# The second mixer's projection, indexer and top-k in one unrolled block

## The reference, cut to what matters

```
z = h @ w_in                      # 1024 q | 512 k,v | 512 qi | 64 ki | 8 wi
q, k, qi, ki = rope(...)          # on the first 16 of each 64 columns
score = sum_h relu(qi_h . ki / 8) * wi_h     # 8 indexer heads, causal
keep  = top_k(score, 128 of 512)  # sample rows: 64 of 257
o = softmax(q k^T / 8 over keep) v ;  x += o @ w_out
```

## Time and profile before

| | |
|---|---|
| median of 3 runs | 2544.56 us (2543.56 to 2545.28) |
| the profiled execution | 2541.22 us, of which the trace spans 2539.5 us |
| busy: PE, DVE, ACT, POOL | 2351.2, 1109.2, 712.6, 285.3 us |
| page, weight loads of the mixer | 16 of 512 KB, 3.6 us to landing |

### The profile page before, as it was taken

The page is one execution under the profiler, slowest core; times in us unless marked ns, Lnnn a source line. Parts: engine busy times, 40 slices in busy tenths (PEclk is TensorE's granted clock), DMA queues, the critical chain, the costliest instruction groups (busy, mean ns, idle before and its releaser), DMA issues. The chain is left out here.

```text
span 2539.5 us, 43612 instructions
## 1 busy us (share of the span) xinstructions
PE 2351.2 (93%) x17356; PEld 2121.0 (84%) x17356; DVE 1109.2 (44%) x1802; ACT 712.6 (28%) x1179; POOL 285.3 (11%) x356
## 2 busy tenths in 40 slices
PE   6999999988799889999999999999964989999997
PEld 5999998766644689999998999997742468999997
DVE  5433433222477435434434433433277744443434
ACT  2221222222255123222223222222241513222220
POOL 1000002000255120000020000011040412000002
PEclk8999999997899999999999999999976989999998
DMA  3332332225300222332332332332201012332331
GB/s 101 91 102 81 91 102 65 82 63 182 117 18 1 67 67 83 95 96 86 96 91 75 91 100 83 91 100 67 79 28 56 12 29 80 91 102 81 91 102 56
DMA packets 327479, 202.44 MB, mean 80 GB/s; under 512 B 11698, under 2 KB 306666, under 8 KB 327322
## 3 DMA queue, kind: packets, MB, share of 16 engines
q1 hardware_dynamic: 323226, 199.10, 26.6%
q10 hardware_dynamic: 4160, 2.10, 0.3%
HBM read 194.65 MB, written 10.70 MB: 81 GB/s over the span
## 5 line engine op out<-in xcount | busy, mean ns | idle before, releaser
L156 DVE TENSOR_TENSOR w_lo<-w_stage,w_hi 128x1024 fp32r<-128x1024 f32 (+1 forms) x266 | 350.9, 1319 | 850.2 <-ACT w_hi L149 850.2
L149 ACT ACTIVATE w_hi<-w_stage 128x1024 fp32r<-128x1024 f32 (+1 forms) x266 | 301.9, 1135 | 761.5 <-PE y_ps L163 371.2
L161 PE MATMUL gate_ps<-h_hi,w_hi 128*128 128x260 f32 x1408 | 404.2, 287 | 27.0 <-DVE h_lo L184 19.7
L163 PE MATMUL gate_ps<-h_hi,w_lo 128*128 128x260 f32 x1408 | 402.8, 286 | 0.0
L162 PE MATMUL gate_ps<-h_lo,w_hi 128*128 128x260 f32 x1408 | 401.7, 285 | 0.0
L161 PE MATMUL up_ps<-h_hi,w_hi 128*128 128x260 f32 x1408 | 398.2, 283 | 0.0
L161 PE MATMUL y_ps<-a_hi,w_hi 128*128 128x260 f32 x1408 | 397.9, 283 | 0.0
L163 PE MATMUL up_ps<-h_hi,w_lo 128*128 128x260 f32 x1408 | 397.8, 283 | 0.0
L163 PE MATMUL y_ps<-a_hi,w_lo 128*128 128x260 f32 x1408 | 397.5, 282 | 0.0
L162 PE MATMUL y_ps<-a_lo,w_hi 128*128 128x260 f32 x1408 | 397.4, 282 | 0.0
L162 PE MATMUL up_ps<-h_lo,w_hi 128*128 128x260 f32 x1408 | 396.4, 282 | 0.0
(11 more groups left out here) (425 smaller groups left out, 3246.0 us busy)
## 6 DMA issues: line engine op xcount, KB each, us to landing
w_stage<-w_ffn_in SPq DMA_DIRECT2D x176, 512.0 KB, 3.8
w_stage<-w_ffn_out SPq DMA_DIRECT2D x64, 704.0 KB, 4.5
w_stage<-w_nsa_in SPq DMA_DIRECT2D x20, 512.0 KB, 3.5
w_stage<-w_dsa_in SPq DMA_DIRECT2D x16, 512.0 KB, 3.6
w_stage<-w_nsa_out SPq DMA_DIRECT2D x8, 512.0 KB, 3.5
cmp_page<-cache_nsa_cmp SPq DMA_DIRECT2D x16, 256.0 KB, 3.9
nsa_win_rows<-state_nsa_win SPq DMA_DIRECT2D x16, 256.0 KB, 3.7
w_stage<-w_dsa_out SPq DMA_DIRECT2D x8, 512.0 KB, 3.7
```

Source lines behind the costliest of these rows:

```text
L149: act.activation(e.w_hi[slot][:, 0:cols], e.w_stage[slot][:, 0:cols], ACT.Copy).then_inc(e.hi_done, 1)
L156: dve.tensor_tensor(e.w_lo[slot][:, 0:cols], e.w_stage[slot][:, 0:cols], e.w_hi[slot][:, 0:cols].bitcast(F32), ALU.subtract).then_inc(e.lo ...
L161: pe.matmul(out, w_hi, x_hi, start=first, stop=False)
L163: return pe.matmul(out, w_lo, x_hi, start=False, stop=last)
```

## The change

The whole of `projection`, `turn_stage`, `index_prompt` and `index_sample` of the second mixer becomes one block, `dsa_front`, without loops. Units now come in this order: the short unit (ki, wi) first, then 4 units of qi, then q, q, and k with v (`COLS`). TensorE's program calls `between(s)` after each of the first four token tiles of every unit (s = 4 * unit + tile), and there the other work is placed:

```diff
+    COLS = (1536, 0, 512, 1024)
+            load_units(e, sp, u0 + 2, first + 4)
+            for i in range(16):      # SP: page loads, between the loads of units 3 and 4
+                sp.dma_start(pages[:, i, :], ...).then_inc(pages_in.sem, 16)
+            load_units(e, sp, first + 4, first + UNITS + 2)
...
+            def between(s):
+                if s == 2:    turn_rest()
+                elif s == 9:  ki_rot.wait(pe, 4); turn(KEYS, 2048, HD)
+                elif s == 10: sample_weights()
+                elif 12 <= s < 16: turn_pages(s - 12)          # 4 transposes each
+                elif 20 <= s < 24:
+                    (qi_rot_dve if s < 22 else qi_rot).wait(pe, 4)
+                    turn(QI + s - 20, 1536 + (s - 20) * P, P)
+                    if s >= 22: scores(s - 22)
+                elif 24 <= s < 26: scores(s - 22)
+                elif s == 26: turn_sample(QI_SAMPLE, 1536, 4, True)
+                elif 27 <= s < 34 and s % 2: scores(4 + (s - 27) // 2)
+                elif 37 <= s < 44 and s % 2: scores(8 + (s - 37) // 2)
+                elif s == 45: sample_scores()
+                elif s == 47: sample_sum()
+                elif 48 <= s < 52: turn(Q0 + s - 48, ...)
+                elif s == 52: turn_sample(Q0_SAMPLE, 0, 4)
+                elif 56 <= s < 60: turn(Q1 + s - 56, ...)
+                elif s == 60: turn_sample(Q1_SAMPLE, 512, 4)
+            rest_unit()
+            statistics()
+            for v in range(UNITS):
+                for t in range(NT):
+                    tile(v, t)
+                    if t < NT - 1: between(4 * v + t)
```

`scores(p)` makes two heads at once (12 pairs; relu has 4 buffers instead of 2). All transposes share one PSUM bank, `x0`: each waits until the copy of the one before has read it. From unit 7 on the low parts are made by POOL; its program in order (`low` adds the second half of the sample rows' product, `add(n)` one head's scores):

```diff
+            wi; rope of ki; rope_prompt(1792, 4 heads); low(0); rope_sample(8 heads)
+            split(7); split(8)
+            for n in (8, 9, 10, 11, 12, 13): add(n)
+            split(9); add(14); add(15); low(1)
+            split(10)
+            for n in (16, 17, 18, 19): add(n)
+            rope_prompt(0, 4); split(11); rope_prompt(256, 4); rope_sample(8)
+            for n in (20, 21, 22, 23): add(n)
+            split(12); split(13); low(2); rope_prompt(512, 4)
+            split(14); rope_prompt(768, 4); rope_sample(8)
+            split(15); split_lo of the next stage's first unit
+            rope_prompt(1024, 2); low(3); rope_sample(4)
```

DVE makes the low parts of units 0 to 6, half of qi's group and its rope, the sum of tile 1's scores, then `choose(1)`, `choose(2)`, `choose(3)`, and at the end half of k's rope. ACT makes all high parts, relu and weighing, most copies, and evacuates groups 1 to 3 alone:

```diff
+            split(7); pair(2); pair(3); pair(4)
+            split(8); pair(5); pair(6)
+            for t in range(4): evacuate(1, t)
+            split(9); evacuate(1, 4); pair(7)
+            split(10); pair(8); pair(9); split(11); pair(10); pair(11); split(12)
```

After unit 15 come k's evacuation, rope and transposes and SP's five stores of k and v. The top 64 of the sample rows moves into `attention`, one instruction a step:

```diff
+                if aside is not None:
+                    aside(dve, m)     # m = 4..20: MAX8 or MATCH_REPLACE8 on 8 x 257, last the bias
```

More of the change, by code:

```diff
@@ L717, in rope @@
     both = v[:, :, :, 0:16]
-    shape = [P, NT, heads, 16]
+    rows, tiles = x.shape[0], x.shape[1]
+    shape = [rows, tiles, heads, 16]
     c4, s4 = (s.unsqueeze(2).to_broadcast(shape) for s in (cos, sin))
-    tc, ts_ = (s[:, 0:NT * heads * 16].rearrange("p (t h j) -> p t h j", t=NT, j=16) for s in (t_cos, t_sin))
+    tc, ts_ = (s[0:rows, 0:tiles * heads * 16].rearrange("p (t h j) -> p t h j", t=tiles, j=16) for s in (t_cos, t_sin))
     chain(eng.tensor_tensor(tc, both, c4, ALU.mult))
@@ L1719, with low_row_of, dsa_front @@
 IDX_SCALE = N_IDX ** -0.5
-def index_prompt(e, ctx, block, z, qi_t, ki_t, wi, bias, qt):
+def low_row_of(z, col):
+    return z[0:TS, NT - 1, col:col + 512]
+def dsa_front(e, z, qt, kt, bias, s_s):
     nc = e.nc
[L1728 to L1754, removed]
-                for t in range(NT):
[L1756 to L1772, removed]
-                else:
[L1774 to L1836, removed]
@@ L1839, in index_sample @@
[L1839 to L1872, removed]
-            for k in range(4):
-                i = 4 * n + k
-                landed[i % 4].wait(pe, 16 * (i // 4 + 1))
-                m = pe.transpose(k_ps[n % 2][0:HD, k * P:(k + 1) * P], rows[:, i, :], e.ident[:, :])
-            m.then_inc(turned.sem, 1)
-        copied.wait(pe, 4)
-        step.wait(pe, 6)
-        for b in range(TS):
-            pe.matmul(s_ps[0:64, 0:256], qz[:, b * 64:(b + 1) * 64], kt[:, b, :], start=b == 0, stop=b == TS - 1)
-        for b in range(TS):
-            m = pe.matmul(s_ps[0:64, 256:257], qz[:, b * 64:(b + 1) * 64], ki_t[0:HD, 0, TP + b:TP + b + 1],
-                          start=b == 0, stop=b == TS - 1)
-        m.then_inc(ready.sem, 1)
-        relu_done.wait(pe, 1)
-        pe.matmul(o_ps[0:TS, 0:257], w_bd[:, :], relu[:, :], start=True, stop=True).then_inc(summed.sem, 1)
-    @block.scalar
-    def _(act):
-        ready.wait(act, 1)
-        act.activation(relu[:, :], s_ps[0:64, 0:257], ACT.Relu).then_inc(relu_done.sem, 1)
-    @block.vector
-    def _(dve):
-        chain = Chain(dve, step)
-        turned.wait(dve, 1)
-        chain(dve.tensor_tensor(w_m[:, :], w_ps[0:64, :], e.imask[0:64, :], ALU.mult))
-        chain(dve.tensor_reduce(w_col[:, :], w_m[:, :], AX.X, ALU.add))
-        chain(dve.tensor_scalar(w_bd[:, :], e.isel[0:64, :], w_col[:, :], None, ALU.mult))
-        chain(dve.memset(qz[:, :], 0.0))
-        for par in range(2):
-            chain(dve.tensor_copy(qz[:, :].rearrange("p (b s) -> p b s", s=72)[:, :, par:8:2],
-                                  qi_t[par * HD:(par + 1) * HD, :, TP:T].rearrange("p h b -> p b h")))
-        for n in range(4):
-            turned.wait(dve, n + 2)
-            dve.tensor_copy(kt[:, 2 * n:2 * n + 2, :].rearrange("p b s -> p (b s)"), k_ps[n % 2][0:HD, :]).then_inc(copied.sem, 1)
-        choose(dve, 3)
-        summed.wait(dve, 1)
-        chain(dve.tensor_copy(s[:, :], o_ps[0:TS, 0:257]))
-        for _ in range(TOPK_S // 8):
-            chain(dve.max(top[:, :], s[:, :]))
-            chain(dve.match_replace(s[:, :], top[:, :], s[:, :], TAKEN))
-        chain(dve.tensor_scalar(bias_s[:, :], s[:, :], TAKEN / 2, NEG, ALU.is_gt, ALU.mult))
-    for sig in landed:
-        sig.base += 64
-    for sig, n in ((turned, 5), (copied, 4), (ready, 1), (step, 8 + 2 * TOPK_S // 8), (relu_done, 1), (summed, 1)):
-        sig.base += n
@@ new lines, in dsa_front, with by_act, jobs_of @@
+    u0, first = e.stream.start("dsa.rest"), e.stream.start("dsa.qi")
+    rest = DSA_COLS - 2048
+    n_norm, hn, sums = e.norm_n, e.h_n, e.sums
+    COLS = (1536, 0, 512, 1024)
+    GROUPS, UNITS = 4, 16
+    FROM_POOL = 7
+    PAGES, KEYS, QI, QI_SAMPLE, SUM, Q0, Q0_SAMPLE, Q1, Q1_SAMPLE = 2, 1, 6, 10, 11, 12, 16, 17, 21
+    def by_act(job):
+        return job == KEYS or PAGES <= job < PAGES + 4 or (QI <= job < QI + 4 and (job - QI) % 2 == 0) or job >= SUM
+    def jobs_of(act, job):
+        return sum(1 for k in range(job + 1) if by_act(k) == act)
@@ L1922, in dsa_regions @@
+    pads.base += 2
+    packed.base += 1
+    e.h_n += 1
+    e.norm_n += 1
 def dsa_regions(e):
-    projection_regions(e, "dsa", e.w_dsa_in[0], DSA_COLS, 4)
+    view = e.w_dsa_in[0].rearrange("(k p) n -> p k n", p=P)
+    e.stream.add("dsa.rest", 1, lambda pair, side, at: view[:, :, 2048:DSA_COLS], KC * (DSA_COLS - 2048))
+    e.stream.add("dsa.qi", 4, lambda group, side, at: view[:, 2 * side:2 * side + 2, 1536:2048], 1024, 4)
+    e.stream.add("dsa.in", 12, lambda group, side, at: view[:, 2 * side:2 * side + 2, ds(at(group * 512), 512)], 1024, 4)
@@ L1929, in dsa @@
     with ExitStack() as mix:
-        def sb(n, shape, dt=F32, ctx=mix):
-            return ctx.enter_context(nc.sbuf_tensor(f"dsa_{n}", shape, dt))
-        z = sb("z", [P, NT, DSA_COLS])
-        ot, kn = sb("ot", [P, 8, T]), sb("k_new", [P, 2, TS])
-        bias_s, last_rows = sb("bias_s", [TS, 257]), sb("last_rows", [P, 512])
-        sb_ = SampleBuffers(sb("qbd", [P, 2304]), None, sb("o_rows", [P, 256]))
-        projection(e, "dsa", 4, z, 4, DSA_COLS)
-        with ExitStack() as turns:
-            qt, kt = sb("qt", [P, 8, T], ctx=turns), sb("kt", [P, 2, T], ctx=turns)
-            qi_t, ki_t = sb("qi_t", [P, 4, T], ctx=turns), sb("ki_t", [P, 1, T], ctx=turns)
-            wi, bias = sb("wi", [P, NT, N_IDX], ctx=turns), sb("bias", [P, 4, TP], BF16, ctx=turns)
-            jobs = [(lambda t, c=c: z[:, t, 1024 + c * P:1024 + (c + 1) * P], kt[:, c, :], 1.0, "k") for c in range(2)]
-            jobs.append((lambda t: z[:, t, 2048:2112], ki_t[:, 0, :], 1.0, "k"))
-            jobs += [(lambda t, j=j: z[:, t, 1536 + j * P:1536 + (j + 1) * P], qi_t[:, j, :], SCALE, "q") for j in range(4)]
-            kv, ix = (x[0, 0].rearrange(r, p=P) for x, r in ((e.dsa_kv_p, "(t p) c k d -> p t (c k d)"),
-                                                             (e.dsa_idx_p, "(t p) d -> p t d")))
-            stores = [(kv[:, t, :], z[:, t, 1024:1536]) for t in range(4)] + [(ix, z[:, 0:4, 2048:2112])]
-            stores += [(e.dsa_kv_s[0].rearrange("b s c k d -> (b s) (c k d)"), z[0:TS, 4, 1024:1536]),
-                       (e.dsa_idx_s[0].rearrange("b s d -> (b s) d"), z[0:TS, 4, 2048:2112])]
```

(53 more changed lines are left out.)

472 lines of the change are left out of this document (471 added, 1 removed).

## The result

The changed kernel takes 2486.81 us (median of 4 runs, 2482.86 to 2487.11); the kernel before, on the same chip, 2544.76 (2543.56 to 2545.28). The ratio is 0.9769, with a 95% interval of 0.9752 to 0.9786: 58 us less, against 58 forecast. The profiled execution took 2487.11 us, its span is 2485.3, its clock 0.966; for that execution 2483 was forecast.

What follows compares the result with a forecast made beforehand. TensorE bounds the projection, then DVE's path holds 103.2 us. Products 113.8, insertions 26.5, stalls 7.4, the tail and clock 1 end the front at 157 instead of 217; -60 + 2 gives 2483, median 2486, range 2472 to 2514.

Steps and rivals of the forecast that it cites:

- The bound and its move: Projection bound by TensorE, then 103.2 us on DVE's path, 63 of them top-k; the change puts one under the other.
- The total: Whole kernel: -60 in the front and +2 in the attention give 2483 us for the profiled execution, median 2486.
- Inserted TensorE work, 26.5: Transposes, scores and small products moved between the projection's products, onto TensorE's path: 26.5 us, the change's main cost.
- Stalls, 7.4: TensorE's waits at units 3, 4, 6, 8, 11 and 12 of the projection: sum 7.4 us, bounds 0 and 28 more.
- Units 11 and 12: Projection units whose splits hang on POOL: TensorE waits 0.4 us at the first and 2.2 at the second.
- Rival 4: Waits in the hand-written order stop TensorE 2 us in each of 16 units: +25, 2511 us; chance 0.12.
- Rival 1: POOL is the bound from unit 9 on; at half more per operation 28 us come on top, 2514; chance 0.12.
- Clock, +1: Products between first product and last k tile: 1 us added (0 to 7) for half clock after TensorE's stalls.
- Rival 2: TensorE stays at half clock after stalls of units 8 to 12; units 7 to 15: +74, 2560 us; chance 0.04.
- Top-k hidden, 7.6 spare: DVE's third top-k ends at 139, last k tile ready at 146.6: 7.6 us spare, the 63 us cost nothing.
- Tail, 8.2: After TensorE's end at 147.7: last evacuation, ropes on POOL and DVE, SP's five stores and barrier, until 155.9.
- Attention and warm-up, +2 (0 to 8): 17 small DVE instructions join steps 4 to 20 of the attention: +2 us, bounds 0 and +8.

## Why the prediction was right, step by step

- **The bound and its move.** Right, and shown: with the top-k alone put back the gain is nil.
- **The total.** For the profiled execution 2483 was forecast and 2487.1 measured; 3.9 us of that stood ahead of the first product. The median came out at 2486.8 against 2486 because the profiled execution of before lay 3.3 us under its median, which the sum adds, and that of after 0.3 above its own. So the hit to 1 us is luck; what was right are the stages below.
- **Inserted TensorE work, 26.5.** 28.6 by difference: 149.8 - 113.8 - 5.7 of waits - 1.7 of clock. The rows themselves are cheaper than I had them. Four transposes take 0.36 up to the next product, not 0.56: the 0.70 of five in the earlier trace rows held the step into a score (four take 0.52 up to a score). Scores take 0.63, 0.85 and 1.06, where 0.64, 0.88 and 1.06 were assumed. What I didn't price is the seam. Timeline of PE around a score:

```profile
1837.14 0.40 PE L163 MATMUL dsa_z_ps<-w_hi,dsa_h_lo 128*128 128x512 f32 x1
1837.47 1.13 PE L1994 MATMUL dsa_pair_ps<-dsa_ki_t,dsa_qi_t 64*128 64x512 f32 x4
1838.53 0.50 PE L161 MATMUL dsa_z_ps<-w_hi,dsa_h_hi 128*128 128x512 f32 x1
1838.87 0.40 PE L162 MATMUL dsa_z_ps<-w_lo,dsa_h_hi 128*128 128x512 f32 x1
```

  Product to product is 0.23; product to score is 0.33 and the first product after it takes 0.34. That is 0.2 us at each of 12 scores and about 0.1 at each of 17 groups of transposes, 4 us. Start to start of the inserted rows I sum 23.5; seams bring 27.5, and 1 us is found in no row.
- **Stalls, 7.4.** 5.7. Unit 3's was 2.1 + 0.2 (1.9 forecast) and unit 8's 1.6 (1.9), each by the mechanism named. Units 11 and 12 were over-priced: 2.6 forecast, 0.8 measured. POOL was no faster than I had it: split 12 ended 118.3 after the first product, against 116.5. But TensorE came to it at 117.6 instead of 114.3, because of the seams and the clock. Late TensorE work and a wait for POOL cover each other, and I had added them. Rival 4 needed a wait in each unit; there were four at units 3, 4, 8 and 12 and two small ones. Rival 1 counts 11 splits on POOL where the program has 10 (the row's x10), which no term of the sum used.
- **Clock, +1.** 1.7, in one piece of 3.4 us right behind the page wait. Rival 2 needed it in eight units; it didn't come.
- **Top-k hidden, 7.6 spare.** 8.46, and shown by the ten extra MAX8.
- **Tail, 8.2.** 7.15. The ropes were over-priced: from the last evacuation to the stores POOL took 4.5 us (1887.4 to 1891.9), where 5.8 were forecast. Taking the stores away saves 2.1.
- **Attention and warm-up, +2 (0 to 8).** +1.45 and +1.0. The first is the sample top-k (gone when that moves). The second isn't that: the warm-up goes by how much of it lies at half clock. That is 5.75 us in the changed kernel (6.39 long), 3.68 in the kernel before (5.40), 3.65 with the pages behind unit 4's weights (5.39) and 3.41 in the three kernels with the stores out of the way (5.29).

The sum's errors were +2.1, -1.7, +0.7, -1.1 and +0.5; that they cancel to half a microsecond is luck, that each is small isn't.

## To carry to other kernels

When one engine's serial chain follows a stage in which it idles, the chain's whole length can be had, if the added work of the engine that bounds the stage is counted as full cost. Moving a block of loads in a queue moves its wait to whatever stands behind it; cut the block into pieces that fit between two deadlines instead. Once the chain is hidden, look for the rest in what the next barrier waits for (stores that nobody there needs) and in the few instructions that went to a place without slack.
